# A two-layer encoder step: the layer loop written out, and the SwiGLU's row blocks cut 4, 6, 6, 6 instead of 6, 6, 6, 4

## The reference, cut to what matters

```python
for l in range(DEPTH):
    ...                                   # norm, projections, two attentions, output projection
    xp = xp + mix_output(o_a, o_lat, w_uv[l], gn_a[l], gn_b[l], w_out[l])
    xp = xp + swiglu(xp, ffn_norm[l], w_gate[l], w_up[l], w_down[l])

def swiglu(x, g, w_gate, w_up, w_down):   # 1024 -> 2816 -> 1024
    n = rms_norm(x, g)
    return (jax.nn.silu(n @ w_gate) * (n @ w_up)) @ w_down
```

## Time and profile before

| | before |
|---|---|
| median of 3 runs | 1614.78 us (1612.4 to 1615.67) |
| the profiled execution's own time | 1614.81 us |
| its span, first to last instruction | 1613.5 us |
| PE busy | 1480.8 us, 92% of the span |
| DVE, ACT, POOL busy | 951.4, 663.5, 177.0 us |
| mean granted PE clock | 0.96 |

### The profile page before, as it was taken

One profiled execution on the slowest core, in us unless ns is written; L12 is line 12 of the kernel. 1 busy time (PEld: TensorE's weight loads), 2 busy tenths in 40 slices (PEclk: granted clock), 3 DMA queues, 4 the chain that ended last, 5 costly groups with the idle time before them and its releaser, 6 DMA issues.

```text
span 1613.5 us, 26565 instructions
## 1 busy us (share of the span) xinstructions
PE 1480.8 (92%) x9510; PEld 1388.9 (86%) x9510; DVE 951.4 (59%) x1582; ACT 663.5 (41%) x1292; POOL 177.0 (11%) x121
## 2 busy tenths in 40 slices
PE   3997778899999999999989777889999999999997
PEld 3877666799899999999968666668999999999997
DVE  5257545476955846746633864446587476475565
ACT  2255535433423523524425463353244244253344
POOL 5123300220000000000110440021200000000004
PEclk7997989899999999999999988998999999999999
DMA  3222012023232232321123201131314223133112
GB/s 130 77 91 69 14 47 62 27 79 92 61 111 67 84 95 63 95 82 53 51 78 96 71 27 40 28 81 40 105 40 119 59 79 108 57 99 92 60 41 104
DMA packets 150633, 116.01 MB, mean 72 GB/s; under 512 B 14656, under 2 KB 142912, under 8 KB 150464
## 3 DMA queue, kind: packets, MB, share of 16 engines
q1 hardware_dynamic: 150496, 114.23, 23.5%
HBM read 109.43 MB, written 6.62 MB: 72 GB/s over the span
## 4 chain that ended last, share of the span: by engine, by line
PE 69%; DVE 12%; issue 9%; ACT 6%; POOL 3%; DMA 1%; SPq 0%; DVEq 0%; ACTq 0%; POOLq 0%
PE ps L523 25%; PE ps L1086 9%; PE ps L1085 9%; PE ps L1084 9%; PE ps L568 2%; PE ps L570 2%; PE ps L569 2%; ACT whi L1149 1%; POOL pwx L2178 1%; POOL pw L2178 1%; DVE wlo L1593 1%; PE ps L882 1%; PE ps L908 1%; PE ps L795 1%; DVE xT L2093 1%
## 5 line engine op out<-in xcount | busy, mean ns | idle before, releaser
L1593 DVE TENSOR_TENSOR wlo<-wraw,whi 128x1024 fp32r<-128x1024 f32 (+2 forms) x120 | 136.6, 1139 | 227.9 <-ACT whi L1149 227.9
L1149 ACT ACTIVATE whi<-wraw 128x1024 fp32r<-128x1024 f32 (+2 forms) x120 | 108.9, 915 | 272.0 <-PE ps L523 179.9
L1084 PE MATMUL ps<-tth,ringh 128*128 128x320 f32 x576 | 176.8, 307 | 3.1 <-ACT k L1497 1.8
L1086 PE MATMUL ps<-tth,ringl 128*128 128x320 f32 x576 | 178.0, 309 | 0.0
L1085 PE MATMUL ps<-tl,ringh 128*128 128x320 f32 x576 | 177.3, 308 | 0.0
L523 PE MATMUL ps<-hh,whi 128*128 128x320 f32 x704 | 161.3, 310 | 4.5 <-DVE wlo L1593 2.8
L523 PE MATMUL ps<-hh,wlo 128*128 128x320 f32 x704 | 160.4, 309 | 0.0
L523 PE MATMUL ps<-hl,whi 128*128 128x320 f32 x704 | 160.3, 309 | 0.0
L1084 PE MATMUL ps<-tbh,ringh 128*128 128x320 f32 x432 | 133.6, 309 | 1.9 <-DVE ringl L1978 1.9
L1085 PE MATMUL ps<-tbl,ringh 128*128 128x320 f32 x432 | 133.5, 309 | 0.0
L1086 PE MATMUL ps<-tbh,ringl 128*128 128x320 f32 x432 | 133.5, 309 | 0.0
(11 more groups left out here) (370 smaller groups left out, 3355.4 us busy)
## 6 DMA issues: line engine op xcount, KB each, us to landing
raw_gate<-w_gate SPq DMA_DIRECT2D x18, 1024.0 KB, 5.4
raw_up<-w_up SPq DMA_DIRECT2D x18, 1024.0 KB, 5.4
wraw<-w_down SPq DMA_DIRECT2D x48, 384.0 KB, 3.3
wraw<-w_in SPq DMA_DIRECT2D x16, 512.0 KB, 3.6
wraw<-w_out SPq DMA_DIRECT2D x32, 128.0 KB, 2.9
wraw<-w_out SPq DMA_DIRECT2D x16, 256.0 KB, 3.0
wraw<-w_gate SPq DMA_DIRECT2D x8, 512.0 KB, 3.9
wraw<-w_up SPq DMA_DIRECT2D x8, 512.0 KB, 3.8
```

Source lines behind the costliest of these rows:

```text
L1084: mm(o, wh[:, c, :], xh[:, c, :], start=fresh and c == 0, stop=False, skip_group_check=True)
L1086: ins = mm(o, wl[:, c, :], xh[:, c, :], start=False, stop=c == KH - 1, skip_group_check=True)
L1149: run(whi[:, slot(s, unit_width(u))], wraw[:, slot(s, unit_width(u))], ACT.Copy).then_inc(unit_hi.sem, 1)
L1593: vec.tensor_tensor(wlo[:, w], wraw[:, w], whi[:, w], ALU.subtract).then_inc(unit_lo.sem, 1)
```

## The change

The loop over the layers becomes a Python loop, so both layers stand in the program and all semaphore values are constants. DVE then splits the first weight unit of the next layer ahead of the last addition of this one. The row blocks become 4, 6, 6, 6: the first holds the plain tiles alone, and all nine pairs go to the other three. The right sides are spread over the plain tiles and the first `down` units: what belongs to chunk k is made during tile k + 1, and chunk 3 during the first `down` units. The hidden tiles keep slots of their own in `hh` (`row_slot`), the `down` units of the first block use their banks in another order, and PE's waits follow. The pair load of group 1 stands behind the first two `down` loads in SP's queue.

```diff
-TILES = [6, 6, 6, 4]
+TILES = [4, 6, 6, 6]
-TILE0 = [0, 6, 12, 18]
+TILE0 = [0, 4, 10, 16]
-GROUPS_OF = [(0, 2), (2, 8), (8, 14), (14, 18)]
+GROUPS_OF = [(0, 0), (0, 6), (6, 12), (12, 18)]
-DOWN_PAIR = [3, 0, 1, 2, 0, 1, 2, 3]
+DOWN_PAIR = [[0, 1, 2, 3, 0, 1, 2, 3]] + 3 * [[3, 0, 1, 2, 0, 1, 2, 3]]
-    def layers(eng):
-        with eng.Fori(0, DEPTH) as layer:
-            yield layer
+    def row_slot(tile):
+        return tile if tile < PLAIN else (tile - PLAIN) % 6
-        for l in layers(sp):            # and for PE, ACT, DVE, POOL
+        for l in range(DEPTH):
...
-            load_pair(1)
             for blk in range(NBLK):
                 first, end = GROUPS_OF[blk]
                 load_down(blk, 0)
                 load_down(blk, 1)
+                if blk == 0:
+                    load_pair(1)
...
                     pe.wait_ge(unit_lo.sem, unit_lo.at(l, u + 1))
-                    if d == 0 and blk >= 1:
+                    if blk == 0 and d < 4:
+                        pe.wait_ge(scaled.sem, scaled.at(l, 2 * PLAIN - 2 if d < 2 else 2 * PLAIN + d - 3))
+                    elif d == 0:
                         pe.wait_ge(x_new.sem, x_new.at(l, 8 + 8 * blk))
...
             for i in range(PLAIN):                         # ACT
-                if i + 1 < PLAIN:
-                    weight_hi(l, u + 2)
+                weight_hi(l, u + 2)
...
-                if 1 <= i <= 2:
-                    right_high_plain(i)
                 act.wait_ge(scaled.sem, scaled.at(l, 2 * i + 1))
                 run(tg[:, odd, :], tg[:, odd, :], ACT.Silu).then_inc(silu_new.sem, 1)
                 if i == 0:
                     right_high_plain(0)
-                if i <= 2:
-                    right_high_sums(i)
-                if i == PLAIN - 1:
-                    for x in (1, 5, 6):
-                        left_high(0, x)
+                if i >= 2:
+                    right_high_sums(i - 1)
                 act.wait_ge(h_new.sem, h_new.at(l, i + 1))
-                if i + 1 < PLAIN:
-                    weight_hi(l, u + 3)
+                weight_hi(l, u + 3)
                 run(hh[:, i, :], tu[:, odd, :], ACT.Copy).then_inc(h_hi.sem, 1)
-                if i == 2:
-                    right_high_plain(3)
-                    right_high_sums(3)
-            left_high(0, 3)
+                if i == 0:
+                    right_high_sums(0)
+                else:
+                    right_high_plain(i)
...
+                    if blk == 0 and d == 0:                # ACT, down units
+                        right_high_sums(3)
...
-            weight_lo(l, 0)                                # DVE
+            if l == 0:
+                weight_lo(l, 0)
...
                 vec.tensor_tensor(halves(tg[:, odd, :]), ps[:, base:base + 2, 0:HALF], halves(rA[:, :]), ALU.mult).then_inc(scaled.sem, 1)
                 if i == 0:
                     right_rows(0)
-                    right_sums(0)
                 elif i == 1:
-                    right_sums(1)
-                    right_low_plain(1)
-                elif i == 2:
-                    right_sums(2)
-                    right_low_plain(2)
-                    right_rows(3)
-                elif i == 3:
-                    right_low_sums(3)
-                    left_low(0, 1)
-                    left_sums(0, 1)
-                    left_sums(0, 5)
+                    right_low_plain(0)
+                    right_low_sums(0)
+                else:
+                    right_sums(i - 1)
+                    right_low_plain(i - 1)
...
-                if i + 1 < PLAIN:
-                    weight_lo(l, u + 3)
+                weight_lo(l, u + 3)
                 if i == 0:
-                    right_low_plain(0)
+                    right_sums(0)
+                elif i == 1:
                     right_rows(1)
-                    right_low_sums(0)
-                elif i == 1:
+                elif i == 2:
+                    right_low_sums(1)
                     right_rows(2)
-                    right_low_sums(1)
-                elif i == 2:
-                    right_low_sums(2)
-                    right_sums(3)
-                    right_low_plain(3)
...
                 hidden_lo(TILE0[blk] + TILES[blk] - 1, tu[:, 1, :])
+                if blk == 0:
+                    right_low_sums(2)
+                    right_rows(3)
...
                     if d + 2 < NC_:
                         weight_lo(l, u + 2)
+                    if blk == 0 and d == 0:
+                        right_sums(3)
+                        right_low_plain(3)
+                    if blk == 0 and d == 1:
+                        right_low_sums(3)
...
+                    if u == UNITS - 1 and l + 1 < DEPTH:
+                        weight_lo(l + 1, 0)
                     dve.wait_ge(unit_used.sem, unit_used.at(l, u + 1))
```

More of the change, by code:

```diff
@@ L550, in _ @@
             ins.then_inc(tile_turned.sem, 1)
-        for l in layers(pe):
+        for l in range(DEPTH):
             pe.wait_ge(x_new.sem, x_new.at(l, -1))
@@ L1063, in product @@
                         pe.wait_ge(c_new.sem, c_new.at(l, C_NEW[n - 2, 2]))
-                    if first_pair and blk == 0:
-                        pe.wait_ge(scaled.sem, scaled.at(l, 2 * (PLAIN if n % 2 else PLAIN - 1)))
-                    elif first_pair:
+                    if first_pair:
                         pe.wait_ge(x_new.sem, x_new.at(l, reads + {0: 5, 1: 5, 2: 6, 3: 6, 4: 7, 5: 7}[bx if x == 1 else by if x == 5 else bz]))
@@ L1095, in _ @@
                     w = unit_parts(u, P)
-                    b0 = 2 * DOWN_PAIR[d]
+                    b0 = 2 * DOWN_PAIR[blk][d]
                     pe.wait_ge(unit_lo.sem, unit_lo.at(l, u + 1))
-                    if d == 0 and blk >= 1:
+                    if blk == 0 and d < 4:
+                        pe.wait_ge(scaled.sem, scaled.at(l, 2 * PLAIN - 2 if d < 2 else 2 * PLAIN + d - 3))
+                    elif d == 0:
                         pe.wait_ge(x_new.sem, x_new.at(l, 8 + 8 * blk))
@@ L1155, in _ @@
             run(nh[:, c, :], turned, ACT.Copy, scale=gv[:, G_NEXT + c:G_NEXT + c + 1]).then_inc(n_hi.sem, 1)
-        for l in layers(act):
+        for l in range(DEPTH):
             last = NC_ - 1
@@ L1524, in emptied @@
                         act.wait_ge(up_c21.sem, up_c21.at(l, pair + 1))
-                    run(hh[:, (PLAIN + 2 * pair + j) % 6, :], tu[:, j, :], ACT.Copy).then_inc(h_hi.sem, 1)
+                    run(hh[:, row_slot(PLAIN + 2 * pair + j), :], tu[:, j, :], ACT.Copy).then_inc(h_hi.sem, 1)
             for i in range(PLAIN):
                 odd, u = i % 2, U_FFN + 2 * i
-                if i + 1 < PLAIN:
-                    weight_hi(l, u + 2)
+                weight_hi(l, u + 2)
                 if i == 0:
@@ L1611, in _ @@
                 low(nl[:, c, :], xT[:, c, :], gv[:, G_NEXT + c:G_NEXT + c + 1], nh[:, c, :]).then_inc(n_lo.sem, 1)
-        for l in layers(dve):
+        for l in range(DEPTH):
             steps[0] = 0
@@ L1918, in hidden_lo @@
                 dve.wait_ge(h_hi.sem, h_hi.at(l, f + 1))
-                vec.tensor_tensor(hl[:, f % 6, :], source, hh[:, f % 6, :], ALU.subtract).then_inc(h_lo.sem, 1)
+                vec.tensor_tensor(hl[:, row_slot(f), :], source, hh[:, row_slot(f), :], ALU.subtract).then_inc(h_lo.sem, 1)
             def right_rows(k):
@@ L2021, in _ @@
                 odd, u, base = i % 2, U_FFN + 2 * i, 4 * (i % 2)
-                if i + 1 < PLAIN:
-                    weight_lo(l, u + 2)
+                weight_lo(l, u + 2)
                 if i >= 1:
@@ L2032, in _ @@
                     right_rows(0)
-                    right_sums(0)
                 elif i == 1:
-                    right_sums(1)
-                    right_low_plain(1)
-                elif i == 2:
-                    right_sums(2)
-                    right_low_plain(2)
-                    right_rows(3)
-                elif i == 3:
-                    right_low_sums(3)
-                    left_low(0, 1)
-                    left_sums(0, 1)
-                    left_sums(0, 5)
+                    right_low_plain(0)
[3 more added lines that the diff above has]
+                    right_low_plain(i - 1)
                 dve.wait_ge(unit_used.sem, unit_used.at(l, u + 2))
                 vec.tensor_tensor(halves(tu[:, odd, :]), ps[:, base + 2:base + 4, 0:HALF], halves(rA[:, :]), ALU.mult).then_inc(scaled.sem, 1)
-                if i == PLAIN - 1:
-                    left_low(0, 5)
                 dve.wait_ge(scaled.sem, scaled.at(l, 2 * i + 2))
@@ L2052, in _ @@
                 vec.tensor_tensor(tu[:, odd, :], tu[:, odd, :], tg[:, odd, :], ALU.mult).then_inc(h_new.sem, 1)
-                if i + 1 < PLAIN:
-                    weight_lo(l, u + 3)
+                weight_lo(l, u + 3)
                 if i == 0:
-                    right_low_plain(0)
+                    right_sums(0)
+                elif i == 1:
```

(16 more changed lines are left out.)

## The result

The kernel after took 1590.47 us (median of four runs, 1589.07 to 1594.31) against 1613.59 (1612.08 to 1615.67) for the kernel before beside it: a ratio of 0.9849 with an interval of 0.9832 to 0.9866. Timed again later it was 1591.20 against 1614.85, 0.9863 (0.9844 to 0.9881).

The account below looks back on a forecast made before the run. PE, busy for 92% of the span, was taken as the bound, so gains come from its waits and half clock. 1614.8 - 8.0 - 6.1 - 1.1 + 0 + 1.2 - 0.5 = 1600.3 us; range 1594 to 1609.

Parts of the forecast that it names:

- The edge (A): Between the layers: PE's idle time and low clock nearly go, 8.0 us saved once, bounds 4 and 8.4.
- the last block (B): With six tiles a unit, three PE waits go: 3.05 us a layer, 6.1 in all, bounds 3 and 7.
- the end (C): At the kernel's end the last addition no longer starts late: 1.1 us saved.
- The row of 1.65 us: ACT's wait at the loop's line between the layers, expected to go; keeping some 1.5 us would have given 1601.1.
- The start of the SwiGLU (D): Waits leave the plain tiles but return behind them, 5.4 us against 5.5: nothing gained, before the clock's price.
- the drop of the clock: After the 3.1 us wait in the first `down` unit, half clock costs 0.6 us a layer, bounds 0 and 6.8.
- the hops of 0.2: Hand-over times of 0.2 us in the series of operations making the fourth hidden tile ready behind the plain tiles.
- Constants in place of registers (E): In the waits of all engines: constants save 0.5 us, bounds 0 and 3.
- The edge keeps no wait: Judges the rival that ACT's first split between the layers stays 2.9 us late: 1604 us, chance 0.10.
- The units behind the third don't wait: Judges the rival that all first-block units wait, five more by 0.9 us each: 1609 us, chance 0.14.
- "Slower": Rival: the 3.1 us wait and later short ones keep the first block at 1.2 GHz: 1652 us, chance 0.04.
- The load of `down` 2 did come late behind the megabyte: Judges the no-change rival: that load in the first block lands 7 us late in both layers, 1614 us, chance 0.04.

Follow-up runs that it names:

- e6: The kernel before with a prefetch hint for the branch closing the layer loop, on all five engines: 1610.82 us, 0.9978.
- e4: The kernel after with constants in its waits but each layer inside a loop of one turn: 1591.48 us, 0.9858.
- e8: The kernel after with the layer's number in a register on ACT, DVE and POOL, PE and SP keeping constants: 1597.80 us, 0.9895.
- e12: The kernel after with registers on ACT, DVE and POOL, all wait values worked out before an operation's first wait: 1595.96 us, 0.9890.
- e1: The kernel before with only its layer loop written out: 1607.16 us, 0.9963 to the kernel before.
- e7: The kernel after with the layer's number in a register on PE alone: 1590.10 us, 0.9862.
- e11: The kernel after with the layer's number in a register on DVE alone: 1594.24 us, 0.9872.
- e13: The kernel after with the layer's number in a register on ACT alone: 1591.88 us, 0.9869.
- e2: The kernel after with its layer loop kept, so registers in the waits and no early split: 1602.24 us, 0.9930.
- e5: The kernel after, written out straight, with the layer's number in a register on every engine: 1596.80 us, 0.9898.
- e9: The kernel after with ACT's and DVE's order around the last plain tile changed against the three waits left: 1590.21 us, 0.9859.

## Why the prediction was right and wrong

**The edge (A), the last block (B), the end (C)** were right: 8.33 us for 8.0, no wait in the last block, 1.05 for 1.1. The row of 1.65 us was rightly taken over the price of a branch: told of the jump ahead of time, the 1.65 us become 0.02 (e6). The Trainium skill ("Advanced Engine Details and Errata", Control Flow Timing) prices the branch itself; no run here shows that price, and in e4, whose branch falls through, the edge takes 2.64 us for 2.66. The Trainium skill ("Runtime: NRT & Kernel Launch", Instruction fetch mechanics) says what the row may have held: a taken branch to code outside what is loaded has to fetch it first. e6 agrees.

**The start of the SwiGLU (D)** was right in its places and too dear. Three waits came where they were put, 3.27 us together for 5.1, and the drop of the clock, 0.6 a layer, did not come. Both follow from the step that failed: the hops of 0.2 and the rows of DVE's queue were read from a kernel with registers. With the registers of ACT and DVE left in (e8), the wait is 2.71 and the clock drops, for 3.4 us where 6 were forecast.

**Constants in place of registers (E) is the step that failed.** It said that "the register instructions run while the engine's earlier instruction still does", 0.5 us, at most 3. Against the kernel after, registers on ACT, DVE and POOL cost 6.6 us (median beside median), on PE nothing. Of that the SwiGLU has 2.5 (440.76 and 440.78 against 439.19 and 439.80), and e12 shows that it goes when no register instruction carries a wait. There the step's sentence holds for the first register instruction of an operation, which has no wait, and fails for the ones behind it: at the split of `down` 1 they run only when the product is there, 0.16 us for two. The Trainium skill ("Perfetto Trace Analysis", Per-engine timelines) has the reason: an instruction that the sequencer handles alone sits out its wait in the sequencer, while a DVE or ACT operation is passed on to a queue and waits there. The two rows of ACTq in e8's chain agree.

**The attention** had no term at all, since the diff rearranges nothing in it; but writing out the loop changes every wait there. It gave 6.25 us between the two profiles, and it gave them because both of its attentions were long before and both short after. Part of that is luck: the kernel after again has one of each. Part goes with the registers, which have 12 long of 14 for 6 of 18; e8 without the SwiGLU's 2.5 and e12 put it at 4.1 and 4.8 us by the medians. The waits of PE ahead of the stretch that decides are the same to 0.04 us in the long and the short ones, so it is not a longer wait there that lets the clock fall. By what way the registers make it fall more often, in e12 too, and why e1 shows only 1.5 on the schedule of before, is open.

With A and C as measured (8.33 and 1.05), B and D together as the SwiGLU gained them with registers (before less e8: 7.05) and E at 6.6 the sum is 23.0, and 23.1 and 23.7 were measured. It proves nothing further, since E is the difference between two of these kernels, and B was not measured apart from D.

**The rivals.** The edge keeps no wait. The units behind the third don't wait. "Slower" had its mechanism, but at 3.4 us of half clock and only with registers. The load of `down` 2 did come late behind the megabyte: in the kernel after it lands at 431.17, 6.8 us after its issue (3.3 in the earlier trace rows), and is split at 432.48. So 1.3 us were left of a cover that I had called ample.

## What to carry to other kernels

An edit that changes every instruction's form has to be priced in every stage, not only where the diff moves work. Where an operation has two or three waits on register values, look which of them ends last: if a register instruction carries it, it and those behind it lie on the chain, at the hand-over here 0.08 us each. Then see whether a longer pause of PE costs it the clock. Where a wait goes away, look at once for the DMA that now comes last, and where it stands in its queue.

## What the runs showed of the hardware

- Behind waits of PE of 1.57 to 2.36 us in the first `down` unit (e7, the kernel after, e12, e11, e13) the granted clock stayed at 1.00; behind waits of 2.54, 2.55 and 2.71 (e2, e5, e8) PE ran at half clock, in e8 at 0.50 over 3.4 us. That is no rule for other places: in the attention the same waits of 1.39, 0.88 and 2.10 us went with a clock of 1.00 in one execution of the kernel after and of 0.65 in another.
- An attention took 247.1 to 248.4 us or 250.1 to 253.6. The long ones, 12 of 14 with registers on DVE and 6 of 18 with constants, have more of PE's busy time at half clock and no more idle time: in e8's second layer it was idle for 37.4 us, in that of the kernel after for 39.9.
- A register instruction that carries a wait ran when the wait had ended: in e8 two of them followed the product on ACT, 0.04 us each and 0.08 apart.
- A `down` load of 256 KB behind the pair load of 1024 KB came so late that ACT, free for it, stood idle for 4.38 us (e9); in the kernel after it landed 6.8 us after its issue.
